# One-core transformer blocks: norm statistics with tiles added on VectorE, and weight splits put between the steps of a head's norm

## The chip, the cores and the metric

The kernel runs on one core of a Trainium2 chip, in one launch. The metric is the device time of one execution in microseconds (us); the time of a kernel is the median of its runs.

## The reference

Two blocks for 256 tokens of width 1024 in float32. What the change touches is two norms:

```python
# retention branch, 4 heads, V width 512 per head; o: (B, S, heads, 512)
o = o * lax.rsqrt(jnp.mean(o * o, axis=-1, keepdims=True) + NORM_EPS)
o = (o.reshape(B, S, RET_WIDTH) * gn_g.astype(jnp.float32)).astype(h.dtype)
return (jax.nn.silu(gate) * o) @ w_out

# second block: gated value, causal convolution of 31 taps over 512 channels, layer norm
ya = a_val * jax.nn.sigmoid(a_gate)
ya = causal_dwconv(ya, w_dw_a[l], b_dw_a[l])
ya = jax.nn.silu(layer_norm(ya, ln_a_g[l], ln_a_b[l]))
ya = ya @ w_pw_a[l]
```

Between and around them stand latent attention, two gated updates, a multi-scale pool branch (`u_pool` averaged over windows, then multiplied by `w_pool`), a merge of both branches, and a gated feed-forward part of width 2816 (22 tiles of 128) with a convolution of 3 taps.

## The kernel before

**Layout.** Features lie on the 128 partitions and tokens along the free dimension: an activation of 1024 features is 8 tiles of 128x256. Each engine has its own program, ordered by hand, and the engines meet at semaphores only.

**Weights.** They come in blocks of 128x1024 floats (512 KB), numbered through the whole program: `B_HEAD` (12 per head), `B_RO`, ..., `B_WG` (16 gate blocks), `B_POOL`, `B_PW` (4 pointwise blocks), `B_WO`, `B_UP`, `B_DN`. A block goes through a ring of 4 slots (`RING`): SyncE (SP) loads `raw`, ScalarE copies its high part to `whi` (line 977), VectorE takes the low part `wlo` = `raw` - `whi` (line 1504), and TensorE multiplies high x high, high x low and low x high (lines 475 to 477), 24 products for a strip of 128 output features. `split(b)` is written with the number of the block that TensorE is about to use, and works on the block three further on (`AHEAD` = 3). SP may load a slot again once its low part is taken (`lo_done`), ScalarE may write `whi` once TensorE is through with the slot (`pe_done`). A few strips are multiplied plainly in float32 from `raw` (`plain_tokens`, line 510), without a split; their slot is loaded again when TensorE is through.

**A retention head** has blocks 0 to 3 (Q and K strips), 4 to 7 (V, `head_rest`), 8 to 11 (gate strips; with j the block in the head). Behind strips 8 and 9 the outputs of the head are formed in two banks; ScalarE squares them into SQ (line 1195, semaphore `gsq`). TensorE sums the four tiles of squares over the partitions by four matmuls with `ones` (line 724, M1), between strips 10 and 11, and releases ScalarE's square root (line 1198, `gstat`, `groot`). The gates come from two evacuations of strips (line 1135). VectorE forms gate x output x gain in `gated` (line 1757, tiles 0 and 1 early, 2 and 3 late), the reciprocal (line 1790), the normalised tiles (line 1793, `yf_ready`); ScalarE copies the high half Yh (line 1201, `yh_ready`) and VectorE takes the low half Yl (line 1795, `y_ready`). Behind that both engines split three blocks for the next head. In the second head POOL computes angles for the latent attention, started by the first head's `y_ready`.

**The conv norm.** VectorE applies 31 taps to 4 tiles (line 1983). TensorE runs 12 plain gate strips beside it, then sums the 4 tiles of CO by four matmuls with `ones` (`conv_mean`, line 598), multiplies strip 12, sums the 4 tiles of squares (`conv_squares`, line 606), multiplies strips 13 to 15, the pool block, and then the pointwise blocks, the first two of which write into the banks that ScalarE frees by its gate evacuations (line 1135). VectorE centres the tiles (line 2034), ScalarE squares (line 1390), takes the root (line 1394), VectorE the reciprocal (line 2041) and the product (line 2044), ScalarE applies Silu (line 1400) and copies the high half (line 1403).

**The up projection.** In `up_pass` VectorE applies two older taps to each tile (line 2150) between splits; ScalarE supplies the newest tap and needs their result.

## Time and profile before

| | |
|---|---|
| median of 3 runs | 862.01 us (860.55 to 864.08) |
| the profiled execution: its time, its span | 863.25 us, 861.6 us |
| TensorE busy, mean granted clock | 846.0 us (98%), 0.994 |
| VectorE, ScalarE, POOL busy | 660.5, 458.7, 51.7 us |
| loaded from HBM | 167.95 MB, 196 GB/s over the span |

Span is the time from the first to the last instruction on the engines. A busy engine is one that has an instruction under way; matmuls are pipelined, so that the rows of TensorE overlap and the distance from start to start is what one costs. A matmul in float32 from plain tiles is two records in the trace, one of high and low parts is one. A bracket at the end of a row of the timeline gives the idle time before it and who ended it. The granted clock is given as a share of 2.4 GHz.

### The profile page before, as it was taken

How to read it: one execution, taken by the hardware profiler on the slowest of the kernel's cores; microseconds unless marked ns; L12 is line 12 of the kernel's file. 1: busy time of each engine (PE TensorE's matmuls, PEld its weight loads, DVE VectorE, ACT ScalarE, POOL GpSimd, SP SyncE). 2: the span in 40 equal slices, each digit the busy share in tenths (PEclk: the TensorE clock that was granted, in tenths of full speed). 3: DMA queues.
4: the chain of work that ended last, by engine and by line, in shares of the span. 5: the costliest groups of instructions: out<-in, count | busy, mean ns of one | idle time of the engine just before them, and what ended most of it. 6: DMA issues, size and time to landing. Idle time of an engine off the chain costs nothing.

```text
span 861.6 us, 15244 instructions
## 1 busy us (share of the span) xinstructions
PE 846.0 (98%) x5500; PEld 770.6 (89%) x5500; DVE 660.5 (77%) x962; ACT 458.7 (53%) x685; POOL 51.7 (6%) x61
## 2 busy tenths in 40 slices
PE   9999999999999999999999999999899999999996
PEld 9899999988878999999988789988898999999884
DVE  7879778686966787786866777998698787887565
ACT  6454544554646566657555546102743777677441
POOL 0028000000012000000000000070000000000000
PEclk9999999999999999999999999999999999999998
DMA  8857575669635757473838662444554455556551
GB/s 272 310 190 229 204 232 197 217 240 373 223 104 167 240 169 242 130 264 104 272 129 311 218 222 95 128 150 157 182 183 159 168 205 188 173 195 221 191 170 49
DMA packets 48430, 169.59 MB, mean 197 GB/s; under 512 B 5634, under 2 KB 6402, under 8 KB 48388
## 3 DMA queue, kind: packets, MB, share of 16 engines
q1 hardware_dynamic: 40468, 142.70, 48.7%
q10 hardware_dynamic: 7920, 26.32, 8.8%
q8 instruction: 27, 0.44, 0.2%
q14 instruction: 15, 0.12, 0.1%
HBM read 167.95 MB, written 1.05 MB: 196 GB/s over the span
## 4 chain that ended last, share of the span: by engine, by line
PE 92%; DVE 3%; DMA 2%; issue 1%; ACT 1%; DVEq 0%; ACTq 0%; SPq 0%
PE bank L475 14%; PE bank L476 14%; PE bank L477 13%; PE bank L542 9%; PE bank L544 9%; PE bank L543 9%; PE bank L510 6%; PE bank L488 3%; PE bank L696 2%; PE bank L697 1%; PE bank L698 1%; PE bank L585 1%; PE bank L823 1%; PE bank L841 1%; PE bank L615 1%
## 5 line engine op out<-in xcount | busy, mean ns | idle before, releaser
L977 ACT ACTIVATE whi<-raw 128x1024 fp32r<-128x1024 f32 (+1 forms) x233 | 241.0, 1040 | 222.3 <-PE bank L477 100.3
L1504 DVE TENSOR_TENSOR wlo<-raw,whi 128x1024 fp32r<-128x1024 f32 (+1 forms) x233 | 280.0, 1214 | 93.4 <-ACT whi L977 91.6
L475 PE MATMUL bank<-H,whi 128*128 128x256 f32 x792 | 228.0, 288 | 0.4 <-DVE wlo L1504 0.3
L476 PE MATMUL bank<-H,whi 128*128 128x256 f32 x792 | 224.5, 283 | 0.0
L477 PE MATMUL bank<-H,wlo 128*128 128x256 f32 x792 | 224.5, 283 | 0.0
L475 PEld LDWEIGHTS bank<-H,whi 128*128 128x128 f32 x792 | 152.5, 193 | 1.4 <-issue 0.6
L476 PEld LDWEIGHTS bank<-H,whi 128*128 128x128 f32 x792 | 152.4, 192 | 0.2
L477 PEld LDWEIGHTS bank<-H,wlo 128*128 128x128 f32 x792 | 152.3, 192 | 0.0
L542 PE MATMUL bank<-whi,Y 128*128 128x512 f32 x216 | 84.2, 390 | 0.0
L544 PE MATMUL bank<-whi,Y 128*128 128x512 f32 x216 | 84.1, 389 | 0.0
L543 PE MATMUL bank<-wlo,Y 128*128 128x512 f32 x216 | 84.0, 389 | 0.0
L1520 DVE SCALAR_TENSOR_TENSOR ada_acc<-ada_raw,siluc,ada_acc 128x1024 f32<-128x1024 f32 x46 | 60.1, 1306 | 13.5 <-DMA ada_raw<-ada_in 12.2
L1983 DVE SCALAR_TENSOR_TENSOR WK<-WK,cols 128x256 f32<-128x256 f32 x120 | 55.6, 531 | 0.4
L475 PE MATMUL bank<-Y,whi 128*128 128x256 f32 x176 | 52.1, 296 | 0.0
L476 PE MATMUL bank<-Y,whi 128*128 128x256 f32 x176 | 49.8, 283 | 0.0
L477 PE MATMUL bank<-Y,wlo 128*128 128x256 f32 x176 | 49.8, 283 | 0.0
L510 PE MATMUL bank<-Z,raw 128*128 128x256 f32 x224 | 48.5, 379 | 0.0
L544 PEld LDWEIGHTS bank<-whi,Y 128*128 128x128 f32 x216 | 40.5, 188 | 8.5
L543 PEld LDWEIGHTS bank<-wlo,Y 128*128 128x128 f32 x216 | 40.6, 188 | 8.3
L542 PEld LDWEIGHTS bank<-whi,Y 128*128 128x128 f32 x216 | 40.5, 188 | 8.3
L510 PEld LDWEIGHTS bank<-Z,raw 128*128 128x128 f32 x224 | 42.5, 190 | 5.7
L542 PE MATMUL bank<-whi,H 128*128 128x512 f32 x112 | 44.4, 396 | 0.1
(269 smaller groups left out, 1376.4 us busy)
## 6 DMA issues: line engine op xcount, KB each, us to landing
ada_raw<-ada_in ACTq DMA_DIRECT2D x48, 512.0 KB, 5.1
raw<-w_head SPq DMA_DIRECT2D x47, 512.0 KB, 4.7
raw<-w_up SPq DMA_DIRECT2D x42, 512.0 KB, 3.3
raw<-w_down SPq DMA_DIRECT2D x22, 512.0 KB, 4.3
raw<-w_uq SPq DMA_DIRECT2D x24, 384.0 KB, 3.1
raw<-w_ret_out SPq DMA_DIRECT2D x16, 512.0 KB, 5.4
raw<-w_mla_gate SPq DMA_DIRECT2D x16, 512.0 KB, 4.6
raw<-w_mla_out SPq DMA_DIRECT2D x16, 512.0 KB, 5.0
```

Source lines behind the costliest of these rows:

```text
L475: mm(o, whi[:, s, c], a[:, 0, :], start=start, stop=False)
L476: mm(o, whi[:, s, c], a[:, 1, :], start=False, stop=False)
L477: last = mm(o, wlo[:, s, c], a[:, 0, :], start=False, stop=stop)
L488: last = mm(o[:, tok(t)], raw[:, s, c], WT[:, t, c], start=(k == 0), stop=(k == 7))
L510: last = mm(o.rearrange("p (t m) -> p t m", t=2), raw[:, s, c], WT[:, :, c], start=(k == 0), stop=(k == 7))
L542: mm(o, a[:, k0 + k, 0, tok(t)], hi[:, c], start=start and k == 0, stop=False)
L543: mm(o, a[:, k0 + k, 0, tok(t)], lo[:, c], start=False, stop=False)
L544: last = mm(o, a[:, k0 + k, 1, tok(t)], hi[:, c], start=False, stop=stop and k == 1)
L977: activation(parts_of(b, n)[0], block_in(b, n), ACT.Copy).then_inc(hi_done, 1)
L1504: tt(lo, block_in(b, n), f32(hi), ALU.subtract).then_inc(lo_done, 1)
L1520: stt(ada_acc[:, a, :], ada_raw[:, n, :], siluc[:, bass.ds(2 * i + 2 * o + n, 1)], ada_acc[:, a, :] if before is None else before, ALU.mul ...
L1983: stt(CO[:, c, :], x, w_tap, CO[:, c, :], ALU.mult, ALU.add).then_inc(conv_tap[c], 1)
```

## The change

In the head, VectorE adds the four tiles of squares to one (a 128x512 add, then a 128x256 add, semaphore `gsum`), TensorE takes one matmul with `ones` in place of four, and takes it behind strip 11 in place of before it. Both ScalarE and VectorE put the next head's splits between the steps of the norm. In the conv norm, VectorE adds the four conv tiles to one (`CS`, `conv_sum`) for a single matmul, and adds the squares to two tiles for two matmuls, which stand behind strip 13 in place of strip 12; splits 11 and 12 of the gates move behind the centring, and ScalarE takes the pooled tile earlier and squares before split 12. In the first pass of the up projection one split moves ahead of the second tile pair's taps.

```diff
+        CS = WK[:, 13:15, :]
...
-            def conv_mean(tiles):
+            def conv_mean():
 
                 pe.wait_ge(g_ready, 2)
-                for k in tiles:
-                    pe.wait_ge(conv_tap[k], CONV_K)
-                    last = mm(M2[:, 0:T], ones[:], CO[:, k, :], start=(k == tiles[0]), stop=(k == tiles[-1]))
-                last.then_inc(mean_psum, 1)
+                pe.wait_ge(conv_sum, 2)
+                mm(M2[:, 0:T], ones[:], CS[:, 0, :], start=True, stop=True).then_inc(mean_psum, 1)
 
             def conv_squares():
 
-                for k in range(4):
-                    if k % 2 == 0:
-                        pe.wait_ge(sq_ready, k // 2 + 1)
-                    last = mm(M3[:, 0:T], ones[:], SQ[:, k, :], start=(k == 0), stop=(k == 3))
+                pe.wait_ge(conv_sum, 3)
+                for k in range(2):
+                    last = mm(M3[:, 0:T], ones[:], SQ[:, k, :], start=(k == 0), stop=(k == 1))
                 last.then_inc(stat_ready, 1)
...
-                pe.wait_ge(gsq, 2 * i + 2 * n0 + 2)
-                for t in range(4):
-                    last = mm(M1[:, 0:T], ones[:], SQ[:, t, :], start=(t == 0), stop=(t == 3))
-                last.then_inc(gstat, 1)
                 strip(B_HEAD + 12 * n0 + 11, halves(b)[1], H, 12, i)
+                pe.wait_ge(gsum, 2 * i + 2 * n0 + 2)
+                mm(M1[:, 0:T], ones[:], SQ[:, 0, :], start=True, stop=True).then_inc(gstat, 1)
...
-            conv_mean((0, 1, 2, 3))
+            conv_mean()
             for j in range(12, 16):
...
                 strip(B_WG + j, halves(b)[j % 2], H)
-                if j == 12:
+                if j == 13:
                     conv_squares()
...
                 evac(B_HEAD + 11, 1, SG[:, 2:4, :], ACT.Silu, 12, i)
+                for j in range(12, 14):
+                    split(B_HEAD + j, 1024, 12, i)
                 act.wait_ge(yf_ready, i + 1)
                 activation(dyn(Yh, 4 * i, 4), YF, ACT.Copy).then_inc(yh_ready, 1)
-                for j in range(12, 15 if more else 14):
-                    split(B_HEAD + j, 1024, 12, i)
+                if more:
+                    split(B_HEAD + 14, 1024, 12, i)
...
+            act.wait_ge(pooled, 4)
+            activation(Sh, PO, ACT.Copy).then_inc(pooled_hi, 1)
             evac(B_WG + 9, 0, pair(G, 4), ACT.Sigmoid)
             for j in range(9, 12):
                 split(B_WG + j)
             evac(B_WG + 11, 1, pair(G, 5), ACT.Sigmoid)
-            split(B_WG + 12)
-            act.wait_ge(pooled, 4)
-            activation(Sh, PO, ACT.Copy).then_inc(pooled_hi, 1)
             for p in range(2):
                 act.wait_ge(centred, p + 1)
                 activation(pair(SQ, p), pair(Z, p), ACT.Square).then_inc(sq_ready, 1)
             table(ACT.Sqrt)
+            split(B_WG + 12)
             split(B_WG + 13)
...
                         gated(0, M3)
                         gated(1, M3)
+                        dve.wait_ge(gsq, 2 * i + 2)
+                        tt(pair(SQ, 0), pair(SQ, 0), pair(SQ, 1), ALU.add).then_inc(gsum, 1)
+                        dve.wait_ge(gsum, 2 * i + 1)
+                        tt(SQ[:, 0, :], SQ[:, 0, :], SQ[:, 1, :], ALU.add).then_inc(gsum, 1)
...
                 gated(3, M2).then_inc(o_free, 1)
+                split(B_HEAD + 12, 1024, 12, i)
...
                 tt(YF, YF, over(rstd[:], 4), ALU.mult).then_inc(yf_ready, 1)
+                split(B_HEAD + 13, 1024, 12, i)
...
-                for j in range(12, 15 if more else 14):
-                    split(B_HEAD + j, 1024, 12, i)
+                if more:
+                    split(B_HEAD + 14, 1024, 12, i)
...
-            for j in range(9, 12):
-                split(B_WG + j)
+            for c in range(4):
+                dve.wait_ge(conv_tap[c], CONV_K)
+            tt(CS, pair(CO, 0), pair(CO, 1), ALU.add).then_inc(conv_sum, 1)
+            dve.wait_ge(conv_sum, 1)
+            tt(CS[:, 0, :], CS[:, 0, :], CS[:, 1, :], ALU.add).then_inc(conv_sum, 1)
+            split(B_WG + 9)
+            split(B_WG + 10)
...
-            split(B_WG + 12)
+            split(B_WG + 11)
+            dve.wait_ge(sq_ready, 2)
+            tt(pair(SQ, 0), pair(SQ, 0), pair(SQ, 1), ALU.add).then_inc(conv_sum, 1)
             dve.wait_ge(pooled_hi, 1)
             tt(Sl, PO, f32(Sh), ALU.subtract).then_inc(pooled_ready, 1)
+            split(B_WG + 12)
             split(B_WG + 13)
...
                 older_taps(0)
+                split(B_UP + 4 * o + 3, 1024, 4, i)
                 if not o:
                     older_taps(1)
-                split(B_UP + 4 * o + 3, 1024, 4, i)
```

Two places in the order of the engines' instructions. The first is VectorE at the end of a head: the gated products (G<-bank,cols,G), the reciprocal, the normalised tiles (G<-G,rstd), the low half (Y<-G,Y) and the splits (wlo). Before:

```order
L1757 SCALAR_TENSOR_TENSOR G<-bank,cols,G 128x256
L1789 REGISTER_ALU
L1790 RECIPROCAL rstd<-root 128x256 [waits groot]
L1793 TENSOR_TENSOR G<-G,rstd 128x1024 [waits o_free,grs]
L1795 ISA [waits yh_ready]
L1795 TENSOR_TENSOR Y<-G,Y 128x4x256
L1503 REGISTER_ALU
L1504 TENSOR_TENSOR wlo<-raw,whi 128x1024 [waits hi_done]
L1503 REGISTER_ALU
L1504 TENSOR_TENSOR wlo<-raw,whi 128x1024 [waits hi_done]
L1503 REGISTER_ALU
L1504 TENSOR_TENSOR wlo<-raw,whi 128x1024 [waits hi_done]
```

With the change:

```order
L1756 SCALAR_TENSOR_TENSOR G<-bank,cols,G 128x256
L1502 REGISTER_ALU
L1503 TENSOR_TENSOR wlo<-raw,whi 128x1024 [waits hi_done]
L1793 REGISTER_ALU
L1794 RECIPROCAL rstd<-root 128x256 [waits groot]
L1797 TENSOR_TENSOR G<-G,rstd 128x1024 [waits o_free,grs]
L1502 REGISTER_ALU
L1503 TENSOR_TENSOR wlo<-raw,whi 128x1024 [waits hi_done]
L1800 ISA [waits yh_ready]
L1800 TENSOR_TENSOR Y<-G,Y 128x4x256
L1502 REGISTER_ALU
L1503 TENSOR_TENSOR wlo<-raw,whi 128x1024 [waits hi_done]
```

Of the three splits that stood last, one now stands ahead of the reciprocal, one ahead of the low half, and one behind it.

The second is the conv norm, on ScalarE, from the gate evacuation of strip 9: splits (whi), the pooled tile (S), the squares (WK<-Z), the root. Before:

```order
L1135 ACTIVATE G<-bank 128x512 [waits pe_done]
L977 ACTIVATE whi<-raw 128x1024 [waits pe_done,raw_loaded2]
L977 ACTIVATE whi<-raw 128x1024 [waits pe_done,raw_loaded3]
L977 ACTIVATE whi<-raw 128x1024 [waits pe_done,raw_loaded0]
L1135 ACTIVATE G<-bank 128x512 [waits pe_done]
L977 ACTIVATE whi<-raw 128x1024 [waits pe_done,raw_loaded1]
L1387 ACTIVATE S<-ada_acc 128x4x256 [waits pooled]
L1390 ACTIVATE WK<-Z 128x512 [waits centred] x2
L994 ACT_TABLE_LOAD
L994 ACTIVATE warm<-ones 128x1
L977 ACTIVATE whi<-raw 128x1024 [waits pe_done,raw_loaded2]
L1394 ACTIVATE root<-bank,cols 128x256 [waits stat_ready]
```

With the change:

```order
L1381 ACTIVATE S<-ada_acc 128x4x256 [waits pooled]
L1132 ACTIVATE G<-bank 128x512 [waits pe_done]
L974 ACTIVATE whi<-raw 128x1024 [waits pe_done,raw_loaded2]
L974 ACTIVATE whi<-raw 128x1024 [waits pe_done,raw_loaded3]
L974 ACTIVATE whi<-raw 128x1024 [waits pe_done,raw_loaded0]
L1132 ACTIVATE G<-bank 128x512 [waits pe_done]
L1388 ACTIVATE WK<-Z 128x512 [waits centred] x2
L991 ACT_TABLE_LOAD
L991 ACTIVATE warm<-ones 128x1
L974 ACTIVATE whi<-raw 128x1024 [waits pe_done,raw_loaded1]
L974 ACTIVATE whi<-raw 128x1024 [waits pe_done,raw_loaded2]
L1393 ACTIVATE root<-bank,cols 128x256 [waits stat_ready]
```

The pooled tile moved to the front, and the squares moved ahead of the split of raw_loaded1, whose block comes last of the gates. On VectorE in the same place, from the end of the taps, before:

```order
L1504 TENSOR_TENSOR wlo<-raw,whi 128x1024 [waits hi_done] x3
L2034 SCALAR_TENSOR_TENSOR Z<-bank,WK 128x512 [waits mean_psum]
L2034 SCALAR_TENSOR_TENSOR Z<-bank,WK 128x512
L1504 TENSOR_TENSOR wlo<-raw,whi 128x1024 [waits hi_done]
L2037 TENSOR_TENSOR S<-ada_acc,S 128x4x256 [waits pooled_hi]
L1504 TENSOR_TENSOR wlo<-raw,whi 128x1024 [waits hi_done]
L2041 RECIPROCAL rstd<-root 128x256 [waits root_done,centred]
```

With the change:

```order
L2027 TENSOR_TENSOR WK<-WK 128x512 [waits conv_tap2,conv_tap3,conv_tap1,conv_tap0]
L2029 TENSOR_TENSOR WK<-WK 128x256 [waits conv_sum]
L1503 TENSOR_TENSOR wlo<-raw,whi 128x1024 [waits hi_done] x2
L2044 SCALAR_TENSOR_TENSOR Z<-bank,WK 128x512 [waits mean_psum]
L2044 SCALAR_TENSOR_TENSOR Z<-bank,WK 128x512
L1503 TENSOR_TENSOR wlo<-raw,whi 128x1024 [waits hi_done]
L2047 TENSOR_TENSOR WK<-WK 128x512 [waits sq_ready]
L2049 TENSOR_TENSOR S<-ada_acc,S 128x4x256 [waits pooled_hi]
L1503 TENSOR_TENSOR wlo<-raw,whi 128x1024 [waits hi_done] x2
L2054 RECIPROCAL rstd<-root 128x256 [waits root_done,centred]
```

Two adds stand ahead of the splits and one behind the third split; the splits of two more blocks stand behind the centring (Z<-bank,WK).

## Rows read from the trace of the kernel before

**Rows 1.** Page, part 1: engine, busy time, share of the span, instructions.
```profile
PE 846.0 (98%) x5500; PEld 770.6 (89%) x5500; DVE 660.5 (77%) x962; ACT 458.7 (53%) x685; POOL 51.7 (6%) x61
```

**Rows 2.** Chain of waits at the end of each head: start us, us, what.
```profile
86.93 1.73 PE bank L724 x8
...
166.06 1.73 PE bank L724 x8
```

**Rows 3.** PE's waits: line, releaser: us in total, times, longest.
```profile
PE bank L606 <- ACT WK L1390: 2.7, 1, 2.7
...
PE bank L475 <- DVE wlo L1504: 0.3, 1, 0.3
```

**Rows 4.** Groups by line and form: busy us, mean ns, idle before.
```profile
L2131 DVE TENSOR_TENSOR WK<-WK 128x512 f32<-128x512 f32 x11 | 7.5, 685 | 0.0
...
L1534 DVE TENSOR_TENSOR WK<-WK 128x256 f32<-128x256 f32 x8 | 3.4, 426 | 0.4
```

**Rows 5.** VectorE's timeline at the end of the second head: start us, us, instruction.
```profile
83.09 1.63 DVE L1504 TENSOR_TENSOR wlo<-raw,whi 128x1024 fp32r<-128x1024 f32 x1
...
86.98 0.86 DVE L1757 SCALAR_TENSOR_TENSOR G<-bank,cols,G 128x256 f32<-128x256 f32 x2
...
92.29 0.88 DVE L1757 SCALAR_TENSOR_TENSOR G<-bank,cols,G 128x256 f32<-128x256 f32 x2 [3.01 <-ACT G L1135]
...
93.09 1.74 DVE L1790 RECIPROCAL rstd<-root 128x256 f32<-128x256 f32 x1
...
94.86 1.22 DVE L1793 TENSOR_TENSOR G<-G,rstd 128x1024 f32<-128x1024 f32 x1
...
98.61 3.49 DVE L1504 TENSOR_TENSOR wlo<-raw,whi 128x1024 fp32r<-128x1024 f32 x3
```

**Rows 6.** ScalarE's timeline over the same stretch.
```profile
89.33 0.47 ACT L1198 ACTIVATE root<-bank,cols 128x256 f32<-128x256 f32 x1
...
91.56 0.60 ACT L1135 ACTIVATE G<-bank 128x512 f32<-128x512 f32 x1 [0.45 <-PE bank L477]
...
96.22 1.06 ACT L1201 ACTIVATE Y<-G 128x1024 f32 x1 [4.05 <-DVE G L1793]
```

**Rows 7.** Busy time of each engine during the second head.
```profile
46.00:87.00 41.00, 41.00 (x286) 38.55 (x285) 35.39 (x36) 19.44 (x23) 24.11 (x15) 1.00 0.62 204
```

**Rows 8.** TensorE's timeline in the conv norm.
```profile
600.56 1.89 PE L598 MATMUL bank<-WK,ones 128*128 128x256 f32 x8
...
608.06 2.46 PE L606 MATMUL bank<-WK,ones 128*128 128x256 f32 x8 [2.75 <-ACT WK L1390]
```

**Rows 9.** Busy time and granted clock (PEclk) just behind that wait.
```profile
609.00:613.00 4.00, 4.00 (x19) 3.74 (x18) 1.98 (x2) 3.83 (x6) 0.00 (x0) 0.57 0.35 120
```

**Rows 10.** ScalarE's timeline in the conv norm.
```profile
605.49 1.06 ACT L977 ACTIVATE whi<-raw 128x1024 fp32r<-128x1024 f32 x1 [3.23 <-DMA raw<-w_gates]
...
607.40 1.13 ACT L1390 ACTIVATE WK<-Z 128x512 f32<-128x512 f32 x2
...
610.90 0.46 ACT L1394 ACTIVATE root<-bank,cols 128x256 f32<-128x256 f32 x1
...
615.54 1.08 ACT L1400 ACTIVATE Z<-Z,cols 128x256 f32<-128x256 f32 x2
...
621.19 0.60 ACT L1135 ACTIVATE G<-bank 128x512 f32<-128x512 f32 x1
```

**Rows 11.** SyncE's load of the pool weights, and its time to landing.
```profile
601.44 0.34 SPq L337 DMA_DIRECT2D raw<-w_pool_w  x1
...
DMA to landing us min/median/max: 5.3/5.3/5.3
```

**Rows 12.** VectorE's timeline in the conv norm.
```profile
612.17 1.74 DVE L2041 RECIPROCAL rstd<-root 128x256 f32<-128x256 f32 x1
```

**Rows 13.** VectorE's timeline at the start of the up projection.
```profile
679.05 3.25 DVE L2150 SCALAR_TENSOR_TENSOR WK<-WK,cols 128x256 f32<-128x256 f32 x8
...
682.22 3.49 DVE L1504 TENSOR_TENSOR wlo<-raw,whi 128x1024 fp32r<-128x1024 f32 x3
```

More of the change, by code:

```diff
@@ L239, in program @@
         mean_psum, centred, t_ready = sem("mean_psum"), sem("centred"), sem("t_ready")
+        conv_sum = sem("conv_sum")
         tok_done, row_sq, row_root, row_var = sem("tok_done"), sem("row_sq"), sem("row_root"), sem("row_var")
@@ L248, in program @@
         o_ready, o_free = sem("o_ready"), sem("o_free")
-        gsq, gstat, groot, grs = sem("gsq"), sem("gstat"), sem("groot"), sem("grs")
+        gsq, gsum, gstat, groot, grs = sem("gsq"), sem("gsum"), sem("gstat"), sem("groot"), sem("grs")
         yf_ready, yh_ready, y_ready = sem("yf_ready"), sem("yh_ready"), sem("y_ready")
```

## The prediction

> **What bounds the kernel now.** I read the page first: TensorE is busy 846.0 of 861.6 us [rows 1], so only what leaves TensorE's own queue, or ends one of its few waits, can shorten the kernel. Next the waits of TensorE: 2.7 us stand at the squares of the conv norm and 0.3 at a product of the up projection [rows 3]. VectorE and ScalarE are not the bound on average, but VectorE has phases that are nearly full: in the second head it is busy 35.39 of 41 us, because POOL works beside it (24.11 us) [rows 7]. So the added tile sums are free only if VectorE delivers each of them, and each split behind them, before TensorE asks.
>
> **Part 1, the four heads.** Before, one head's statistic is four matmuls of ones by squares; each is two records, and the chain shows 1.73 us for 8 records [rows 2], 0.216 each. There are four such pieces, 39.6 us apart. The change leaves one matmul, two records: 4 x 6 x 0.216 = **5.2 us** less on TensorE, if nothing new waits.
>
> What VectorE pays is one 128x512 add and one 128x256 add: 0.69 + 0.43 = 1.1 us per head by the nearest rows of the same operation and shapes [rows 4]; squares in SBUF are all that they read. Are they in time? In the second head the two gated products end at 86.98 + 0.86 = 87.8 [rows 5], the adds would end at 89.0. The statistic now stands behind the next strip. It used to start at 86.93 [rows 2]; a strip takes 2.9 us (in the conv norm TensorE goes from 600.56 + 1.73 to a wait that begins at 608.06 - 2.75, one strip and a drain, 3.0 [rows 8]), so TensorE asks at 89.8: 0.8 us of margin. In that head it has already gained 1.3 us from the head before, while VectorE, by the paragraph after next, gains some 0.3 only. That makes a wait of about **0.2 us**, once. In the first head the margin is alike and TensorE has gained nothing yet; in the third and fourth, without POOL, VectorE comes earlier. I charge nothing there.
>
> Which way can contention turn this? A split took 1.63 us while POOL ran, against 1.16 in a row of three without it [rows 5]. POOL's run starts when the first head is normalised, which will be later, so it may still run at the adds: 1.1 us would become 1.5, and the split ahead of them longer by the same 0.4. My bounds for the wait are therefore 0 and 1.0 us. The Trainium skill (GPSIMD Engine Reference, section Specifications) says that POOL shares its SBUF interfaces with VectorE, and that instructions with two SBUF inputs contend: the added adds are of that kind, the gated products that read PSUM are not its case. The trace agrees with the rule (1.63 against 1.16 for such a split). By this rule the sum would be up to 0.8 us worse than without contention.
>
> What the norm's later steps do: the square root starts at 89.33 before [rows 6]. The sum now leaves TensorE at 89.8 + 0.4 and the root starts about 90.4, 1.1 later; with its 0.47 and a table load the gate's activation moves from 91.56 to 92.2. Gated products 2 and 3 then start at 93.0 (before 92.29), and end at 93.9. Here the reorder matters. Before, the three splits came last, at 98.61 to 102.1 [rows 5]; the first of them, the fourth strip of the next head, was ready at 99.8, about when TensorE wanted it (86.93 + 1.73 + four strips = 100.2). TensorE now wants it 1.3 us earlier. With the old order and a later root, that would be a wait of some 2 us per head. With the new order the split stands at 93.9 to 95.1, the reciprocal (1.74) ends at 96.9, the multiplication (1.22) at 98.1, the second split at 99.2 (wanted 101.8), then the low half of Y (ScalarE's copy takes 1.06 [rows 6]) to 100.5, and the third split to 101.7 (wanted 104.5). VectorE is through at 101.7, against 102.1 before: it gains 0.3 to 0.4, TensorE 1.3, so margins in the next head shrink by 1.0 and do not shrink further from head to head, since each head waits for TensorE in its middle. On ScalarE the two splits fill a stretch that was idle (4.05 us before the copy of Y [rows 6]). The SP queue gets its buffers earlier by the first split and as early as before by the last. For the last head the output product asks for its low half only after 6 of 8 blocks; nothing is charged. Heads: 5.2 - 0.2 = **5.0 us**.
>
> **Part 2, the conv norm.** The ceiling first. The mean goes from 8 records to 2, the squares from 8 to 4: 10 x 0.216 = 2.2 us. The wait for the squares is 2.75 us with a drain of 0.2. Its cause is not arithmetic: ScalarE stands behind a split whose weights land at 605.49, and takes the squares at 607.40 only [rows 10]. The change puts them ahead of that split, right behind the centring: mean at 601.0, centred at 602.7, squared at 603.4, added at 604.5; TensorE passes at 606.8, a strip later than before. And behind that wait the granted clock averaged 0.57 over 4 us [rows 9], half of the 2.4 GHz for most of it, which cost 4 x 0.43 = 1.7. All together 6.8 us: the first product of the pointwise weights began at 608.06 + 1.7 (squares) + 1.7 (clock) + 4 x 2.9 (three strips and the pool block) = 623.0, and could begin at 600.56 + 1.3 + 5 x 2.9 = 616.3.
>
> It will not, because it needs a bank that ScalarE frees. Follow that chain. Loads are not earlier than before: the pool weights are issued at 601.44 and take 5.3 us [rows 11], so ScalarE splits them at 606.8 to 607.9; the statistic is ready at 607.8; the root runs 607.9 to 608.4 (before 610.90). VectorE splits to 609.1, takes the reciprocal (1.74 [rows 12]) to 610.9 and the first half's product (0.66) to 611.5. From the Silu at 615.54 to the end of the gate's activation, 621.19 + 0.60, there were 6.25 us of ScalarE's own work [rows 10]: it ends at 617.8. The product starts at 618.0, after a new wait of some 1.7 us. The saving is 623.0 - 618.0 = **5.0 us**. Bounds: if ScalarE were not held by the pool weights' landing, the wait would be 0.7 and the saving 6.0; if they land 1 us later, 4.0; if the granted clock falls behind the new wait as it did behind the old one, a further 1.7 is lost. The row shows the fall after 2.75 us without work, while after other waits (all under 1 us) the pitch stayed; 1.7 is nearer to the first than to the second only by a little, and I take no fall. Behind this, the merges on VectorE move 4.1 us earlier with TensorE 5.0: the fourth is ready about 0.5 us ahead of its product. No charge.
>
> **Part 3, the up projection.** In its first pass one split moves ahead of four taps (3.25 us for 8 [rows 13]), so it ends 1.6 us earlier than 683.4. TensorE waited 0.34 for it and lost 0.2 in restarting: **0.5 us**. The taps behind it end at 683.5, when ScalarE reads them anyway.
>
> **Sum.** 5.0 + 5.0 + 0.5 = 10.5 us. The profiled execution took 863.25 us, so it would be 852.75; the median of the runs lies 1.24 below that execution, and I forecast **851.5 us**.
>
> **Rivals.** (a) The granted clock falls behind the new wait in the conv norm. For: it did after 2.75 us; against: this wait is shorter, and only the squares' end is behind it. 851.5 + 1.7 = 853.2. (b) VectorE is late in the head where POOL runs: its margin of 1.0 less is used up at the mask of the scores or at the adds, 1 to 2 us, 853.0. (c) The heads' gain is eaten by splits that come too late in each following head: 1.3 x 3 = 3.9, 855.4. Against: by the working above the splits have 2.5 us of room. (d) The conv norm's gain does not arrive: if its chain to the gate's activation were bound by the loads throughout and moved only 1.2 us, the time would be 855.3; (c) and (d) together 859.2, no change that can be told. (e) Better: ScalarE is freed sooner and no wait remains at the pointwise weights, 849.8. (f) Slower: the wait for the added squares stands in TensorE's queue ahead of the next head's strips. Should the adds come 2.75 us after the strip in each head, the granted clock falls there too, as it did behind the same wait in the conv norm: 4 x (2.75 + 1.7) = 17.8 against the forecast, 869.3. It decides when the adds end about 3.5 us later than I work out; with 1.1 us of adds and idle stretches of 3 us on VectorE right behind them [rows 5] I see no source for that.
>
> **How the numbers follow.** The forecast's own case 0.37; (a) 0.18; (b) 0.14; (c) 0.08; (d) 0.08; (c) with (d) 0.05; (e) 0.07; (f) 0.03. Half a per cent, 4.3 us, is about what a measurement of this kernel can tell from no change. Faster by more than that (under 857.7) are all but the last two of the poorer ones: 0.92; the same 0.05; slower 0.03. The range takes in (e), (a), (b), (c) and (d), with the bounds of 4.0 and 6.0 for the conv norm and about 1 us either way of scatter between runs: 849.0 to 855.6. Outside remain (f), (c) with (d), and edges.
>
> **What would show it.** In the changed profile: the pieces at the heads' ends 0.43 us instead of 1.73, no PE wait on VectorE's adds except a small one in the second head, 38.3 us from head to head; the PE wait at the squares gone, the granted clock full there, and a new wait of 1 to 2 us at the first product of the pointwise weights, released by ScalarE; the wait in the up projection gone. A PE wait on the weights' low parts in a following head would show (c); a granted clock under 1.00 near 612 us would show (a). The forecast is wrong if the span is above 855 or below 848 us.

## The result, and the profile with the change

| | before | with the change |
|---|---|---|
| median of 6 runs each, same chip | 861.28 us (859.65 to 864.08) | **850.79 us** (850.06 to 853.38) |
| ratio, 95% interval | | 0.9881 (0.9861 to 0.9901) |
| span of the profiled execution | 861.6 us | 849.3 us |
| TensorE busy, mean granted clock | 846.0 us, 0.994 | 836.6 us, 0.997 |

The kernel is 10.5 us faster, by the median as much as forecast (851.5 us, 10.5 us less). TensorE has 34 matmul records less, 24 in the heads and 10 in the conv norm (page, part 1, beside [rows 1]):

```profile
PE 836.6 (99%) x5466; PEld 762.5 (90%) x5466; DVE 665.6 (78%) x973; ACT 458.4 (54%) x685; POOL 50.3 (6%) x61
```

Two lines of TensorE's list of waits touch the argument. The 2.7 us at the squares and the 0.3 us in the up projection [rows 3] are gone, and one wait is new, the first:

```profile
PE bank L477 <- ACT G L1132: 0.8, 1, 0.8
PE bank L695 <- DVE wlo L1503: 0.6, 1, 0.6
```

No wait on VectorE's adds is among them. The second line belongs to a place that the change doesn't touch.

**The heads.** The chain of waits, at the first pieces of each head and at the first of the output product (start us, us, what):

```profile
34.44 0.86 PE bank L703 x4
...
72.72 0.86 PE bank L703 x4
...
111.12 0.86 PE bank L703 x4
...
149.40 0.86 PE bank L703 x4
...
164.82 0.43 PE bank L723 x2
165.25 3.57 PE bank L614 x32
```

From head to head it is 38.3 us, as forecast (72.72 - 34.44, 149.40 - 111.12). The same two marks in the kernel before:

```profile
34.82 0.86 PE bank L704 x4
...
170.66 3.57 PE bank L615 x32
```

From the first mark to the output product it is 130.8 us now and was 135.8: the heads gained 5.0. VectorE at the end of the second head, where the margin was thinnest (compare [rows 5]):

```profile
85.86 0.86 DVE L1756 SCALAR_TENSOR_TENSOR G<-bank,cols,G 128x256 f32<-128x256 f32 x2
86.65 0.68 DVE L1785 TENSOR_TENSOR WK<-WK 128x512 f32<-128x512 f32 x1
87.36 0.43 DVE L1787 TENSOR_TENSOR WK<-WK 128x256 f32<-128x256 f32 x1
...
91.13 0.88 DVE L1756 SCALAR_TENSOR_TENSOR G<-bank,cols,G 128x256 f32<-128x256 f32 x2 [2.21 <-ACT G L1132]
91.97 1.23 DVE L1503 TENSOR_TENSOR wlo<-raw,whi 128x1024 fp32r<-128x1024 f32 x1
93.12 1.75 DVE L1794 RECIPROCAL rstd<-root 128x256 f32<-128x256 f32 x1
```

and TensorE's matmul that takes the sum:

```profile
87.98 0.59 PE L723 MATMUL bank<-WK,ones 128*128 128x256 f32 x2
```

The adds end at 87.79 (87.36 + 0.43) and TensorE takes them at 87.98, with no idle time before it: 0.2 us of margin where a wait of 0.2 was forecast. In the other heads the margins were 2.4 to 3.8 us. The three lower rows show the new order: the split stands in the place where VectorE would else have gone straight to the reciprocal.

**The conv norm.** TensorE's sums, and the product at which it now waits (compare [rows 8]):

```profile
594.55 0.59 PE L599 MATMUL bank<-WK,ones 128*128 128x256 f32 x2
...
600.73 1.02 PE L605 MATMUL bank<-WK,ones 128*128 128x256 f32 x4
...
611.21 0.38 PE L477 MATMUL bank<-Y,whi 128*128 128x256 f32 x1 [0.83 <-ACT G L1132]
```

ScalarE over the same stretch (compare [rows 10]):

```profile
594.84 1.06 ACT L974 ACTIVATE whi<-raw 128x1024 fp32r<-128x1024 f32 x1 [2.26 <-DMA raw<-w_gates]
...
596.28 1.14 ACT L1388 ACTIVATE WK<-Z 128x512 f32<-128x512 f32 x2
...
598.84 1.99 ACT L974 ACTIVATE whi<-raw 128x1024 fp32r<-128x1024 f32 x2
601.79 0.47 ACT L1393 ACTIVATE root<-bank,cols 128x256 f32<-128x256 f32 x1 [0.96 <-PE bank L605]
...
610.55 0.60 ACT L1132 ACTIVATE G<-bank 128x512 f32<-128x512 f32 x1
```

The squares stood 6.8 us behind the mean's matmul before (607.40 - 600.56) and stand 1.7 behind it now (596.28 - 594.55), ahead of the splits of the last gate block and of the pool weights (598.84). The root no longer waits behind a split; it waits 0.96 us for TensorE. The pool weights, issued at 595.44, are reported with 4.2 us from issue to landing (5.3 before [rows 11]), so they did not hold ScalarE. On VectorE only split 11 has moved from ahead of the centring to behind it; split 12 stood behind it already. The granted clock is full over the whole norm (busy time by stretch; PEclk is the third value from the end):

```profile
600.00:604.00 4.00, 4.00 (x33) 3.90 (x32) 3.91 (x3) 3.01 (x5) 0.00 (x0) 1.00 0.87 315
```

**Where the 12.3 us between the two spans went.** Four marks of the chain of waits divide what follows the heads: the first plain strip of the second block (line 488 before, 490 with the change), the first and the last plain strips of the up projection (the same line), and a piece of VectorE near the end. Before:

```profile
520.63 3.57 PE bank L488 x32
...
665.07 3.57 PE bank L488 x32
...
673.54 1.80 PE bank L488 x16
...
847.65 0.70 DVE Z L1632
```

With the change:

```profile
514.63 3.57 PE bank L490 x32
...
653.42 3.57 PE bank L490 x32
...
661.88 3.57 PE bank L490 x32
...
835.40 0.70 DVE Z L1631
```

Between the first two stands the conv norm and nothing else that changed: 144.4 us before, 138.8 now, 5.6 less. This stretch is called **the gauge** below. Between the last two stands the up projection and nothing else that changed: 174.1 before, 173.5 now, 0.6 less. With 5.0 in the heads the touched places make 11.2 us. The remaining 1.1 us of the difference lie where the code is the same (0.4 ahead of the first mark of the heads, 0.6 between the output product and the second block's first plain strip, 349.97 against 349.38), and the medians, 10.5 us apart, don't show them.

### The profile page after: what moved, and what is told of

Same layout as the page of the kernel before. It is cut to its first block, busy times and chain, and to the rows that moved or that the text cites. A ratio compares the mean times of both kernels' runs of the same rounds, so it can differ in the third digit from the quotient of the medians.

```text
span 849.3 us, 15189 instructions
## 1 busy us (share of the span) xinstructions
PE 836.6 (99%) x5466; PEld 762.5 (90%) x5466; DVE 665.6 (78%) x973; ACT 458.4 (54%) x685; POOL 50.3 (6%) x61
## 4 chain that ended last, share of the span: by engine, by line
PE 91%; DVE 3%; ACT 3%; DMA 1%; issue 1%; ACTq 0%; SPq 0%; DVEq 0%
PE bank L477 14%; PE bank L478 13%; PE bank L479 13%; PE bank L544 9%; PE bank L546 9%; PE bank L545 9%; PE bank L512 5%; PE bank L490 2%; PE bank L695 2%; PE bank L696 2%; PE bank L697 1%; PE bank L587 1%; PE bank L820 1%; PE bank L838 1%; PE bank L614 1%; PE bank L715 1%
```

## The experiments

My theory before the first of them: the heads give about 5 us because one matmul replaces four and the reordered splits keep up; the conv norm gives about as much because the squares come ahead of a split that waits for its load; the adds matter there for 2.2 us of records only. The rivals: the gain comes from the records alone, or from the order alone; the splits' order is of no account; the clock does the rest. Each ratio below is against the kernel before on the same chip, with its 95% interval. A label is shortened to its number, e1 for e1_heads_only.

**1. The two halves apart.** Label e1_heads_only is the kernel before with the heads' part of the change; e2_conv_only has the conv norm's part. In neither is the up projection changed. The core of the edits, against the changed kernel:

```diff
 # e1_heads_only
-            conv_mean()
+            conv_mean((0, 1, 2, 3))
...
-                if j == 13:
+                if j == 12:
                     conv_squares()
 # e2_conv_only
+                for t in range(4):
+                    last = mm(M1[:, 0:T], ones[:], SQ[:, t, :], start=(t == 0), stop=(t == 3))
+                last.then_inc(gstat, 1)
                 strip(B_HEAD + 12 * n0 + 11, halves(b)[1], H, 12, i)
-                pe.wait_ge(gsum, 2 * i + 2 * n0 + 2)
-                mm(M1[:, 0:T], ones[:], SQ[:, 0, :], start=True, stop=True).then_inc(gstat, 1)
```

> The kernel before with the heads' part of the change alone (tile adds on VectorE, one matmul with ones behind strip 11, the next head's splits between the steps of the norm). My theory: each head's piece of 1.73 us becomes 0.43, no new wait, so 5.0 to 5.2 us less, 856.2 us against 861.3 of before; the conv norm keeps its wait of 2.7 us at the squares and the up projection its 0.3. Rival, that the heads' gain is eaten by late splits in the next heads: 860 us or more, with a TensorE wait on the low parts of the weights. Rival, that the gain of the change is all in the conv norm and the heads are neutral: 861.3.

> The kernel before with the conv norm's part of the change alone (adds, order on ScalarE and VectorE, squares behind strip 13). My theory: the wait of 2.7 us and the low granted clock behind it go, 10 records of 0.216 us go, and a new wait of about 0.8 us stands at the first product of the pointwise weights: 5.8 us less, 855.5 us. The ends of the heads keep 1.73 us each. Rival, that part of the 12.3 us between the two profiled spans is scatter outside the touched places: then this and the heads alone give less than 11 together. If the granted clock falls behind the new wait: 857.2.

Measured: e1 855.77 us (854.54 to 856.72), ratio 0.9936 (0.9923 to 0.9948); e2 856.75 us (855.67 to 856.82), ratio 0.9945 (0.9932 to 0.9958); before 861.25. So 5.5 and 4.5 us, together 10.0, and the halves add up to the whole less the up projection: neither lives on the other. e2 came out 1.2 us above the 855.5 expected, which had been read from one pair of profiles (5.8 us for this norm).

The marks tell the parts apart with less scatter. From the heads' first mark to the output product it is 135.8 us in all four profiles with the old heads (three of the kernel before, e2) and 130.8 in seven with the new ones (the change in two executions, e1, and from below e4, e5, e6 and e12). The gauge of e2 reads 138.8, as with the change. From the third mark to the last it is 174.1 us in all five profiles without the up projection's part (three of before, e1, e2) and 173.5 in seven with it (the change in two, and e3, e4, e5, e6 and e12, all described below): that part gives **0.6 us**, though the medians can't show it.

In e1 the wait at the squares stayed (TensorE's timeline, and the stretch behind it):

```profile
600.98 2.00 PE L606 MATMUL bank<-WK,ones 128*128 128x256 f32 x8 [2.38 <-ACT WK L1390]
```

```profile
602.00:604.00 2.00, 2.00 (x16) 1.90 (x14) 0.05 (x1) 1.99 (x4) 0.00 (x0) 1.00 0.61 231
```

Behind 2.38 us without work the granted clock stayed full, and the gauge read 142.5. That was the first sign that the fall of [rows 9], for which I had counted 1.7 us, is no fixed part of the kernel before.

**2. The splits at the end of the head, as before.** e3_splits_last keeps all adds and single matmuls:

```diff
 # VectorE; ScalarE alike
                 gated(3, M2).then_inc(o_free, 1)
-                split(B_HEAD + 12, 1024, 12, i)
...
                 tt(YF, YF, over(rstd[:], 4), ALU.mult).then_inc(yf_ready, 1)
-                split(B_HEAD + 13, 1024, 12, i)
...
-                if more:
-                    split(B_HEAD + 14, 1024, 12, i)
+                for j in range(12, 15 if more else 14):
+                    split(B_HEAD + j, 1024, 12, i)
```

> The changed kernel, but both engines take the three splits for the next head last again, behind the low half of Y. My theory: the reorder is what lets the heads keep their gain. Without it the fourth strip of the next head finds its low part 1.4 us late (splits begin at about 97.3 in the second head, the strip wants its block at 97.1), in three heads: 4.2 us more than the changed kernel, 855 us, with TensorE waits on wlo of 1 to 2 us each. Rival, that the splits are early enough in either order: 850.8 and no wait.

Measured: 855.5 us (854.92 to 856.56), ratio 0.9932 (0.9919 to 0.9945). TensorE's waits have one more line, and VectorE's timeline at the end of the first head shows why:

```profile
PE bank L477 <- DVE wlo L1501: 4.6, 3, 1.5
```

```profile
58.12 1.23 DVE L1796 TENSOR_TENSOR Y<-G,Y 128x1024 f32 x1 [1.39 <-ACT Y L1198]
59.26 3.69 DVE L1501 TENSOR_TENSOR wlo<-raw,whi 128x1024 fp32r<-128x1024 f32 x3
```

The first of the three splits ends only at about 60.5, and TensorE resumes there after 1.5 us; the second, third and fourth head pay it. From the first mark of the heads to the output product it is 136.0 us (34.52 to 170.53), against 130.8 with the change and 135.8 before: **all that the heads gain is lost**. Fewer matmuls alone are worth nothing here; the moved splits let them through.

**3. The conv norm, adds and order apart.** e5_conv_adds_old_order keeps the adds but puts TensorE's squares and both engines' splits back; e6_conv_order_no_adds keeps the order and sums with four and four matmuls.

```diff
 # e5_conv_adds_old_order
-                if j == 13:
+                if j == 12:
                     conv_squares()
...
             evac(B_WG + 11, 1, pair(G, 5), ACT.Sigmoid)
+            split(B_WG + 12)
+            act.wait_ge(pooled, 4)
+            activation(Sh, PO, ACT.Copy).then_inc(pooled_hi, 1)
 # e6_conv_order_no_adds
-                pe.wait_ge(conv_sum, 3)
-                for k in range(2):
-                    last = mm(M3[:, 0:T], ones[:], SQ[:, k, :], start=(k == 0), stop=(k == 1))
+                for k in range(4):
+                    if k % 2 == 0:
+                        pe.wait_ge(sq_ready, k // 2 + 1)
+                    last = mm(M3[:, 0:T], ones[:], SQ[:, k, :], start=(k == 0), stop=(k == 3))
```

> The changed kernel, but in the conv norm only the adds are kept: ScalarE's and VectorE's order are the ones of before (split 12 and the pooled tile ahead of the squares) and the squares' matmuls stand behind strip 12 again. My theory: the wait at the squares comes from ScalarE standing behind a load, so it stays and even grows by what TensorE arrives earlier (1.3 us) and by the add (0.7): 4 to 5 us, with the granted clock fallen behind it. Saving of the conv norm then below 1 us: 855 to 857 us. Rival, that fewer records are the gain: 2.2 of the 5.8 us remain saved, 854.4.

> The changed kernel, but in the conv norm only the order is kept: four matmuls for the mean and four for the squares, no adds on VectorE. My theory: the mean comes 1.3 us later and with it the whole chain to the gate's evacuation; the wait at the pointwise weights stays near 0.8 or less since TensorE comes 2.2 us later and the chain 1.3 to 2.2: 1.3 to 2.2 us more than the changed kernel, 852.1 to 853.0, no wait at the squares. Rival, that the adds carry the conv norm's gain: 856.

Measured: e5 855.99 us (855.5 to 856.61), ratio 0.9942 (0.9922 to 0.9962); e6 853.25 us (852.82 to 854.15), ratio 0.9915 (0.9894 to 0.9936); before 860.97. e5 lies with the kernel that has the heads alone (855.77): in the conv norm the adds with the old order give nothing. Its TensorE waits, and the stretches that hold that wait and what is behind it:

```profile
PE bank L605 <- DVE WK L2047: 5.0, 1, 5.0
```

```profile
602.00:604.00 2.00, 1.58 (x5) 1.31 (x5) 1.50 (x2) 1.99 (x3) 0.00 (x0) 0.50 0.67 244
604.00:606.00 2.00, 2.00 (x10) 1.91 (x9) 1.87 (x2) 1.55 (x3) 0.00 (x0) 0.50 0.00 0
```

The squares still stand behind the late split, and the add behind them lengthens the wait from 2.4 to 5.0 us; the clock went to half. The gauge reads 145.0. In e6 it reads 141.0, with the same 0.8 us wait at the pointwise weights as the change and none at the squares. 141.0 - 138.8 = 2.2 us is just the 10 records; the rest of the conv norm's gain is order. e5 puts the whole order back, so which of its moves is needed is not separated: with TensorE's squares alone one strip (2.9 us) later, some 2.1 of the 5.0 us of wait would be left, an estimate that no run tests.

**4. What if the adds came late?** e7_adds_held_back (one execution) puts four 128x1024 products on VectorE ahead of the adds of each head; nobody reads what they write.

```diff
                         gated(1, M3)
+                        for d in range(4):
+                            if d:
+                                dve.wait_ge(held, 4 * i + d)
+                            tt(WK[:, 12:16, :], maskd[:], maskd[:], ALU.mult).then_inc(held, 1)
                         dve.wait_ge(gsq, 2 * i + 2)
```

> The changed kernel with four idle products of 128x1024 on VectorE (1.17 us each, 4.7 in all) ahead of the adds in each head. It measures the margin and what a wait there costs. In the changed kernel the adds end 2.4, 0.2, 3.8 and 3.8 us ahead of TensorE in the four heads, so waits of 2.3, 4.5, 0.9 and 0.9 us on VectorE are expected at line 723's matmul. My theory: the granted clock stays full behind the short ones and falls for about 4 us behind those above 2.7, which costs a further 1.7 each. Rival, that a wait costs its own length only: the granted clock stays 1.00 in all heads. Sum: 8.6 us of waits, with later splits on top, and 1.7 to 3.4 of clock: 861 to 864 us.

Measured: 861.7 us, the whole gain of the change gone (before on the same chip: 859.3 to 862.5). TensorE's waits, its row in the second head, and the granted clock behind it:

```profile
PE bank L724 <- DVE WK L1792: 8.5, 4, 4.6
```

```profile
95.29 0.74 PE L724 MATMUL bank<-WK,ones 128*128 128x256 f32 x2 [4.63 <-DVE WK L1792]
```

```profile
54.00:56.00 2.00, 2.00 (x19) 2.00 (x18) 0.63 (x2) 1.99 (x3) 0.00 (x0) 1.00 0.72 254
...
96.00:98.00 2.00, 2.00 (x11) 2.00 (x11) 0.37 (x1) 1.91 (x3) 0.00 (x0) 0.50 0.22 51
```

The waits were 2.21, 4.63, 0.80 and 0.85 us in the four heads. The first row is the stretch behind the 2.21: full clock. Behind 4.63 it fell to half. So the mechanism of rival (f) exists, and with VectorE 5 us later than it is, it takes back the gain; clearly slower than before the kernel was not even then.

**5. POOL beside the adds.** In the change POOL's run has ended before the adds of the second head, which left the case of contention untested. e8_pool_at_the_adds (one execution) starts it at the second head's squares:

```diff
             pool.wait_ge(trig_arg, 1)
+            pool.wait_ge(gsq, 3)
             pool.wait_ge(y_ready, 1)
```

> The changed kernel with POOL's computation of the angles started by the second head's squares in place of the first head's Y, so that it runs from about 82 to 106 us, across the adds and splits of the second head's norm. If POOL slows VectorE's instructions with two inputs in SBUF, the adds take more than the 0.68 and 0.43 us of the changed kernel, and splits 1.4 to 2.3 in place of 1.22, in that stretch, while the stretch from 60 to 82 runs at full rate; the gated products, which read a bank, stay at 0.43 each. The margin at the adds (0.2 us) is then either won back by the faster stretch ahead (2 us more) or lost. Rival, no contention: all durations as elsewhere. Time near 851 in both.

Measured: 849.98 us. POOL's share over the stretch, and VectorE's timeline in it:

```profile
82.00:102.00 20.00, 20.00 (x158) 19.49 (x157) 14.38 (x14) 11.16 (x12) 18.87 (x14) 1.00 0.43 146
```

```profile
82.58 0.69 DVE L1785 TENSOR_TENSOR WK<-WK 128x512 f32<-128x512 f32 x1
83.31 0.58 DVE L1787 TENSOR_TENSOR WK<-WK 128x256 f32<-128x256 f32 x1
...
90.65 0.87 DVE L1756 SCALAR_TENSOR_TENSOR G<-bank,cols,G 128x256 f32<-128x256 f32 x2 [3.38 <-ACT G L1132]
...
92.64 1.75 DVE L1794 RECIPROCAL rstd<-root 128x256 f32<-128x256 f32 x1
94.42 2.12 DVE L1797 TENSOR_TENSOR G<-G,rstd 128x1024 f32<-128x1024 f32 x1
...
98.01 2.34 DVE L1800 TENSOR_TENSOR Y<-G,Y 128x1024 f32 x1
```

Operations that read two tiles of SBUF are stretched: the small add from 0.43 to 0.58, the product from 1.22 to 2.12, the low half from 1.23 to 2.34. The gated products, which read PSUM, and the reciprocal, which reads one tile, keep 0.87 and 1.75. The Trainium skill (GPSIMD Engine Reference, section Specifications) names instructions with two SBUF inputs as those that contend with POOL. These rows agree in that only such instructions are stretched; how much is lost, from nothing (the 128x512 add, 0.69 against 0.68) to nine tenths, differs from operation to operation. No wait of TensorE came of it: the adds end at 83.9 and are taken at 87.50, since VectorE's work ahead of them now ran without POOL (33.02 us busy from 46 to 87, against 35.72 in the change). The contention costs 0.15 us at the adds against a margin of 3.6; all four heads together took 131.1 us against 130.8.

**6. A better order in the conv norm.** e4_root_first takes the added squares behind strip 12 again, adds them ahead of VectorE's split, and takes the root ahead of ScalarE's split of the pool weights. VectorE's low half of the pooled tile and its split of the pool weights move behind the reciprocal and the products (not in the cut below):

```diff
-                if j == 13:
+                if j == 12:
                     conv_squares()
...
             split(B_WG + 12)
-            split(B_WG + 13)
             act.wait_ge(stat_ready, 1)
             activation(root[:], M3[:, 0:T], ACT.Sqrt, bias=col("ln_eps"), scale=1.0 / (4 * P)).then_inc(root_done, 1)
+            split(B_WG + 13)
...
-            split(B_WG + 11)
             dve.wait_ge(sq_ready, 2)
             tt(pair(SQ, 0), pair(SQ, 0), pair(SQ, 1), ALU.add).then_inc(conv_sum, 1)
+            split(B_WG + 11)
```

> The changed kernel, with the squares' matmuls behind strip 12, the squares' add ahead of a split on VectorE, the root ahead of the pool weights' split on ScalarE, and the reciprocal ahead of the pooled tile's low half on VectorE. My theory: the remaining wait of 0.8 us at the pointwise weights hangs on the chain from the root over the reciprocal and the Silu to the gate's evacuation; this starts it 1.3 us sooner, so that wait goes, and a wait of about 0.4 us appears at the squares: 0.4 us less than the changed kernel, 850.4, seen in the profile rather than in the times. Rival, that this wait hangs on the loads: it stays at 0.8, and the time is 851.2.

> The changed kernel, unchanged, beside before and beside the kernel with the root first, on one chip. Expected: 850.8 us, waits as in its first profile (0.8 at the pointwise weights, none at the squares), granted clock full through the conv norm.

> The kernel with the root first (squares behind strip 12, root and reciprocal ahead of splits), again, beside the changed kernel on one chip. My theory: 0.4 to 0.9 us below the changed kernel, since its profile had no wait in the conv norm at all and the stretch from one transposition's weights to the next was 137.9 against 138.8 us. Rival: the difference of 0.8 between the medians was scatter between chips: no difference.

Measured: e4 849.97 us (849.3 to 850.49), ratio 0.9865 (0.9851 to 0.9880). In the later comparison the changed kernel (e11) took 851.08 us (849.99 to 853.14), ratio 0.9891 (0.9871 to 0.9911), and the root-first kernel (e12) 849.81 us (849.0 to 850.42), ratio 0.9875 (0.9855 to 0.9895). The wait at the pointwise weights is gone from TensorE's list, and ScalarE takes the root at once (timeline of e4):

```profile
599.86 0.45 ACT L1392 ACTIVATE root<-bank,cols 128x256 f32<-128x256 f32 x1
...
609.31 0.60 ACT L1132 ACTIVATE G<-bank 128x512 f32<-128x512 f32 x1
```

Counted from the mean's matmul (594.91 in e4, 594.55 with the change), the root is 2.3 us earlier and the gate's activation, which frees the bank, 1.6 earlier. The gauge reads 137.9 in both executions, against 138.8 in both of the changed kernel. Expected were 0.4 us and a wait of 0.4 at the squares; that wait did not appear. The medians, 0.8 and 1.3 us below, agree with the gauge's 0.9, though the intervals of the ratios overlap; the gauge is the better witness.

**7. The clock in the kernel before.** Two further profiles of that kernel, with no edit:

> The kernel before, unchanged, for a second profile. The heads-only kernel kept the same wait at the squares (2.38 us), and the granted clock behind it stayed at 1.00, where in the first profile of before it fell to 0.57 over 4 us behind 2.75. My theory now: a wait of this length is followed by the fall in some executions and not in others, so that my term of 1.7 us for the clock was an accident of one profile. Then the wait here is 2.4 to 2.8 us again, and the clock behind it is either 1.00 or near 0.5 for up to 4 us, the stretch from the mean to the pointwise weights 20.6 to 20.8 or about 22.4 us. Rival: the fall belongs to the kernel before and is always there.

> As the kernel before again, a third profile of the same kernel. If the granted clock behind the wait at the squares is full in one of the three and fallen in another, the fall is not a property of the kernel, and its 1.7 us must be taken as a chance, not as a term.

e9 took 860.87 us, e10 862.47. TensorE's row at the squares and the stretch 608 to 610 us, first of e9:

```profile
607.25 1.99 PE L606 MATMUL bank<-WK,ones 128*128 128x256 f32 x8 [2.43 <-ACT WK L1390]
```

```profile
608.00:610.00 2.00, 2.00 (x14) 1.86 (x13) 0.13 (x1) 1.99 (x3) 0.00 (x0) 1.00 0.74 274
```

then of e10:

```profile
605.94 3.78 PE L606 MATMUL bank<-WK,ones 128*128 128x256 f32 x8 [2.50 <-ACT WK L1390]
```

```profile
608.00:610.00 2.00, 2.00 (x8) 1.65 (x7) 1.10 (x1) 1.11 (x2) 0.00 (x0) 0.50 0.16 64
```

The same program and nearly the same wait, 2.43 and 2.50 us: once the eight records took 1.99 us at full clock, once 3.78 at half. The gauge reads 142.6 and 145.6, with 144.4 for the execution of [rows 9] between them. With the differences between the waits taken off (0.1 and 0.3 us), the fall cost 2.9 us in e10 and 1.5 in that execution. **Whether the clock falls here differs from execution to execution, and it costs up to 2.9 us when it does.** The change removes the wait, and with it this loss: in the profiles of the changed kernel and of e4 and e12 the clock is full through the norm.

## Why the prediction came out right

| term | forecast | measured |
|---|---|---|
| heads | 5.2 - 0.2 = 5.0 | 5.0 between marks in every profile; 5.5 by e1's medians |
| conv norm | 5.0 | by the gauge 5.6 in the first pair of profiles, 3.8 against e9, 6.8 against e10; 4.5 by e2's medians |
| up projection | 0.5 | 0.6 between marks, wait gone |
| sum | 10.5 | 10.5 by the medians |

*Heads.* Right in size and in mechanism: 0.43 us for a piece that took 1.73, 38.3 us per head. The step "a wait of about **0.2 us**, once" did not happen; the adds were 0.2 us early instead, and e8 shows that the bound of 1.0 us from contention was not reached either. The price of contention had been read from a split of 1.63 us "against 1.16 in a row of three"; the like of 1.63 is a single split of 1.22. Rival (c) was no idle worry: with the old order of splits it happens in full (e3: 1.5 us per head, 4.6 in all). The prediction had said "some 2 us per head" for that order.

*Conv norm, the new wait.* The place and the releaser were right, the size was not: 0.83 us, not 1.7. The step that failed is "take 5.3 us [rows 11], so ScalarE splits them at 606.8 to 607.9": a duration read under the old order was used for the new one. The load took 4.2 us this time and held nobody; what remained was the lower bound, 0.7, where the chain runs through root, reciprocal and Silu alone. In e3 the load took 4.6 us and held ScalarE for 0.26, and the wait was 0.83 all the same. e4, which shortens that chain, removes the wait.

*Conv norm, the clock.* The term "4 x 0.43 = 1.7" was near the 1.5 us of the execution that I read and wrong as a property of the kernel: over three executions of the kernel before the loss was nothing, 1.5 and 2.9 us. What was said of the other waits, "all under 1 us", also overlooked one of 1.3 us (PE bank L578 <- DVE ones L1707). By the medians the norm gives 10.5 - 5.0 - 0.6 = 4.9 us (4.5 in e2). With the wait at its true size the forecast would have been 5.9, so the clock's part was put some 1.0 us too high for the median execution (scatter included) and the new wait 0.9 too high; these two errors cancelled. That the sum hit the measured 10.5 is in that part luck. Rival (a) did not happen: the clock stayed full in the change. Rival (f) needs adds that are some 5 us later (e7), rival (d) needs the loads to bind, which they did not.

*Up projection.* The wait of 0.3 us is gone from the list and the marks give 0.6 us, for the 0.34 of wait and 0.2 of restart that were forecast.

## What to carry to other kernels

Small statistics matmuls on a matrix engine that is 98% busy are a real part of its time, but adds that replace them pay only if what the next stage needs is ready that much earlier: with the splits in their old place the heads gave nothing, with the old order the conv norm gave nothing. Look for work that stands in an in-order queue behind a load that it doesn't need. Read a small gain between two marks of the trace: 0.6 us was the same in every profile, and no median could show it. And price a loss that comes from the clock from more than one execution: here single profiles of the kernel before give anything from 3.8 to 6.8 us for the same edit.

## What was not expected of the hardware

- The granted clock behind a wait of TensorE: full behind 2.21, 2.38 and 2.43 us, fallen to half in or behind 2.50, 2.75, 4.63 and 4.99 us (each seen once). Two executions of one program, whose waits differ by 0.07 us, fell on either side. The moment of the fall differed too: in e5 the clock averaged 0.51 from 600 to 602 us, while TensorE still stood idle, until 602.42; in e7 it averaged 0.95 from 94 to 96 us, though TensorE had stood idle for 4.63 us until 95.29, and was at half only behind that. So the length of the wait alone does not tell; what decides was not tried.
- Under POOL's work two instructions of one kind fared differently: 1.23 to 2.34 us for the low half, 1.22 to 1.35, 1.41 and 1.63 for splits of the same size, 0.68 to 0.69 for the larger add and 0.43 to 0.58 for the smaller. Which of POOL's instructions ran beside each was not resolved.
- The load of the pool weights (512 KB, its place in the queue unchanged) took 4.9 to 5.3 us from issue to landing in all five profiles with the old order of the conv norm (three of before, e1, e5) and 4.0 to 4.6 in all nine with the new one. Why is open; it is no scatter of one profile. Working with the time of the old order misplaced the chain by 0.7 of the 0.9 us by which the new wait was missed.
